# The modulation product of a two-block transformer step: TensorE beside the latent stage, or VectorE beside the feed-forward stage

## The reference, cut to what matters

```python
def _sq_relu_mlp(h, w_ff_in, w_ff_out):
    return jnp.square(jax.nn.relu(h @ w_ff_in)) @ w_ff_out
...
sil_c = jax.nn.silu(c)
sil_cc = jax.nn.silu(c_ctx)
mx = (sil_c @ w_ada[l] + b_ada[l])[:, None, :]
mc = sil_cc @ w_ada[l] + b_ada[l]
xsh1, xsc1, xg1, xsh2, xsc2, xg2 = jnp.split(mx, N_ADA, axis=-1)
csh1, csc1, cg1, csh2, csc2, cg2 = jnp.split(mc, N_ADA, axis=-1)
px = _split_in(_modulate(x, xsh1, xsc1) @ w_in[l])
pc = _split_in(_modulate(ctx, csh1, csc1) @ w_in[l])
```

## Time and profile before

| | us |
|---|---|
| median of 3 runs (4472.01 to 4479.48) | 4474.55 |
| span of the profiled execution, first to last instruction | 4370.0 |
| TensorE busy (84% of the span) | 3684.3 |
| VectorE busy (50%) | 2180.5 |
| GpSimd busy (27%) | 1195.4 |
| ScalarE busy (19%) | 846.3 |

### The profile page before, as it was taken

The page is one execution under the profiler, slowest core; times in us unless marked ns, Lnnn a source line. Parts: engine busy times, 40 slices in busy tenths (PEclk is TensorE's granted clock), DMA queues, the critical chain, the costliest instruction groups (busy, mean ns, idle before and its releaser), DMA issues.

```text
span 4370.0 us, 33503 instructions
## 1 busy us (share of the span) xinstructions
PE 3684.3 (84%) x10958; PEld 1877.5 (43%) x10958; DVE 2180.5 (50%) x4839; ACT 846.3 (19%) x1788; POOL 1195.4 (27%) x1151
## 2 busy tenths in 40 slices
PE   8788899899999799993999997476877678788787
PEld 4345564444445356542654456333433233233222
DVE  0547532310001356895652544885478778544443
ACT  1223321200003222113211122201122122111111
POOL 0200000000000000000000101335377777777775
PEclk9875758999999998995999998788999899999999
DMA  3340011122221111320122235677499999999998
GB/s 152 140 146 1 14 45 39 52 76 75 77 96 58 53 58 53 104 79 29 45 80 76 80 119 192 218 243 273 176 406 368 352 365 385 368 408 409 368 406 320
DMA packets 171916, 765.20 MB, mean 175 GB/s; under 512 B 19256, under 2 KB 19256, under 8 KB 160224
## 3 DMA queue, kind: packets, MB, share of 16 engines
q0 software_dynamic: 157904, 580.06, 35.2%
q1 hardware_dynamic: 13824, 182.97, 11.5%
q10 hardware_dynamic: 16, 0.02, 0.0%
HBM read 744.08 MB, written 18.89 MB: 175 GB/s over the span
## 4 chain that ended last, share of the span: by engine, by line
PE 49%; DVE 20%; POOL 9%; DMA 8%; issue 6%; ACT 3%; POOLq 0%; DVEq 0%; ACTq 0%
PE ps L252 13%; PE ps L258 9%; POOL arena L2589 8%; DMA arena<-in_pu,arena 5%; PE ps L1278 5%; PE ps L1336 5%; DVE arena L2619 5%; DVE arena L1422 4%; PE ps L2542 3%; PE ps L220 3%; PE ps L814 2%; PE ps L1560 2%; PE ps L832 2%; DMA arena<-in_pv,arena 2%; PE ps L1547 1%
## 5 line engine op out<-in xcount | busy, mean ns | idle before, releaser
L2542 PE MATMUL ps<-arena 128*128 128x512 f32 x2048 | 1001.8, 631 | 320.5 <-DMA arena<-in_pv,arena 159.3
L2619 DVE CUSTOM_DVE_ANT_0 arena<-arena 128x1024 f32<-128x1024 f32 x512 | 623.5, 1221 | 377.8 <-DMA arena<-in_pu,arena 376.7
L252 PE MATMUL ps<-arena 128*128 128x512 f32 (+1 forms) x1768 | 759.8, 590 | 31.4 <-ACT arena L2108 24.4
L2542 PEld LDWEIGHTS ps<-arena 128*128 128x128 f32 x2048 | 379.0, 197 | 925.4 <-issue 518.1
L2589 POOL DMA_INDIRECT arena<-in_pu,arena x512 | 540.6, 1056 | 372.3 <-issue 82.8
L2589 POOL DMA_INDIRECT arena<-in_pv,arena x512 | 545.4, 1065 | 193.3 <-issue 107.3
L258 PE MATMUL ps<-arena 128*128 128x512 f32 (+2 forms) x1408 | 527.1, 536 | 3.1 <-DVE arena L1251 0.9
L252 PEld LDWEIGHTS ps<-arena 128*128 128x128 f32 x1768 | 339.0, 193 | 437.4 <-issue 432.2
L220 PE MATMUL ps<-arena 128*128 128x128 f32 (+1 forms) x1094 | 218.1, 339 | 212.6 <-ACT arena L858 70.5
L258 PEld LDWEIGHTS ps<-arena 128*128 128x128 f32 x1408 | 267.8, 190 | 261.8 <-issue 219.4
L263 POOL TENSOR_TENSOR arena<-arena 128x1 f32<-128x1 f32 (+7 forms) x38 | 61.1, 1610 | 1106.8 <-DVE arena L675 396.7
(11 more groups left out here) (328 smaller groups left out, 3037.5 us busy)
## 6 DMA issues: line engine op xcount, KB each, us to landing
arena<-in_w_in SPq DMA_DIRECT2D x27, 2048.0 KB, 8.2
arena<-in_w_ada SPq DMA_DIRECT2D x12, 2048.0 KB, 8.1
arena<-in_w_ff_in SPq DMA_DIRECT2D x8, 2048.0 KB, 7.8
arena<-in_w_ff_out SPq DMA_DIRECT2D x8, 2048.0 KB, 8.0
arena<-in_w_pq SPq DMA_DIRECT2D x8, 2048.0 KB, 8.7
aside<-arena POOLq DMA_DIRECT2D x20, 512.0 KB, 5.9
arena<-in_w_at SPq DMA_DIRECT2D x4, 2048.0 KB, 8.0
arena<-in_w_o SPq DMA_DIRECT2D x4, 2048.0 KB, 8.2
```

Of the source, the lines that this page charges most:

```text
L252: x = t.matmul(PS[:, b, 0:n], hT[:, k, i * 128:(i + 1) * 128], w[:, k, :], start=k == 0, stop=k == nk - 1)
L2542: x = t.matmul(PS[:, b + c, :], DG[n % 4], row(f)[:, 512 * c:512 * c + 512], start=j == 0, stop=j == 127)
L2619: v.tensor_tensor_reduce(row(f), row(f), TT[i], 1.0, 0.0, ALU.mult, ALU.add, DOT[i % 2][:, j:j + 1]).then_inc(*pe.V.step("dot", 128 * i + j))
```

## The change

The product leaves latent and compress and is formed in `ffn`. The panels `w_ada` are loaded between the 12 first panels of the feed-forward layer, one after each. VectorE multiplies a panel with the condition and sums over the 8 blocks of rows: 8 instructions of 128 x 512 for a condition, two conditions for the first four panels, one for the other eight. TensorE then only sums over the 128 partitions, with a vector of ones: for the first four panels 8 products with 128 x 128 weights and 2 moving columns, for the others one product with 2 weight columns and 512 moving ones. The sums of panels 0 to 6 stand in TensorE's program in the middle of the next panel of the first weights, those of 7 to 11 among the second weights, in banks 4 to 7. The waits of the attention for the eight writes go to ScalarE's program after the relus. The sigmoid of the conditions stands before `gather(0)`.

```diff
-        ORDER = ([("w_in", c) for c in range(4)] + [("w_ada", c) for c in range(9)] + [("w_cmp", 0), ("w_cmp", 1)]
...
+        FF = [("w_ff_in", c) for c in range(8)] + [("w_ff_out", c) for c in range(8)]
+        ORDER = ([("w_in", c) for c in range(4)] + [("w_cmp", 0), ("w_cmp", 1), ("scratch", 0), ("w_xk", 0), ("w_xv", 0),
+                                                    ("w_out", 0), ("w_out", 1), ("w_xq", 0), ("w_xo", 0)]
+                 + [p for c in range(12) for p in (FF[c], ("w_ada", c))] + FF[12:]
...
                 if i < 3:
                     project(i + 1)
-                    drain(ada, 4)
...
         def compress_vector(v):
             wait_all(v, lt.P, lt.A, lt.V, lp.A, lp.V)
-            v.wait_ge(*ad.A.at("mod", 3))
-            o = PAR["bsh1"][0]
-            v.tensor_tensor(MOD, MOD, bc(PR[:, o:o + 16], 2), ALU.add).then_inc(*cm.V.step())
-            cm.V.own(v).tensor_scalar(MODf[:, 16:32], MODf[:, 16:32], 1.0, None, ALU.add).then_inc(*cm.V.step("mod"))
...
-        def compress_tensor(t, ada):
-            drain(ada, 1)
+        def compress_tensor(t):
...
             done("w_cmp", 1, cm.P)
-            drain(ada, 10)
             t.wait_ge(*cm.V.at("kc"))
...
         def attn_vector(v):
             wait_all(v, cm.A, cm.P, cm.V)
-            for s in s_row:
-                v.wait_ge(s, 64)
...
+        def ada_sums_tensor(t, c, banks):
+            t.wait_ge(*ad.V.at("acc", c))
+            b = bank(t, banks, ad.A, "row", c)
+            if c < 4:
+                for r in range(2):
+                    for k in range(4):
+                        x = t.matmul(PS[:, b, 8 * r + 2 * k:8 * r + 2 * k + 2], ADA[c % 2][r][:, 128 * k:128 * k + 128], cs("one")[:, 0:2],
+                                     start=True, stop=True)
+            else:
+                x = t.matmul(PS[0:2, b, :], cs("one")[:, 0:2], ADA[c % 2][0], start=True, stop=True)
+            x.then_inc(*ad.P.step("row", c))
...
+        def ada_sums_vector(v, c):
+            w = w3("w_ada", c)
+            v.wait_ge(*loaded("w_ada", c))
+            if c > 1:
+                v.wait_ge(*ad.P.at("row", c - 2))
+            for k in range(8):
+                ad.V.own(v)
+                for r in range(ada_conditions(c)):
+                    o, s = ADA[c % 2][r], SC[:, k, r:r + 1]
+                    if k == 0:
+                        v.tensor_scalar(o, w[:, k, :], s, None, ALU.mult).then_inc(*ad.V.step("acc", c))
+                    else:
+                        v.scalar_tensor_tensor(out=o, in0=w[:, k, :], scalar=s, in1=o, op0=ALU.mult, op1=ALU.add
+                                               ).then_inc(*ad.V.step("acc", c))
+            done("w_ada", c, ad.V)
+            if c == 4:
+                v.wait_ge(*ad.A.at("row", 3))
...
                     mm_feat(t, b, HT, 8, w3("w_ff_in", c), a, 512).then_inc(*ff.P.step("h", 4 * c + a))
+                    if c and a == 1:
+                        ada_sums_tensor(t, c - 1, BANKS)
...
+                        if c == 0 and i == 1:
+                            ada_sums_tensor(t, 7 + kk, (4, 5, 6, 7))
+                        if c == 0 and kk == 3 and i == 3:
+                            ada_sums_tensor(t, 11, (4, 5, 6, 7))
...
                 a.activation(AT[:, f, :], PS[:, held(ff.A, "h", f), :], ACT.Relu).then_inc(*ff.A.step("h", f))
+                if f > 4 and f % 4 == 1:
+                    ada_sums_scalar(a, f // 4 - 1)
+            for c in range(7, 12):
+                ada_sums_scalar(a, c)
+            for s in s_row:
+                a.wait_ge(s, 64)
+            a.wait_ge(*ad.V.at("mod"))
...
                 v.tensor_tensor(AT[:, f, :], AT[:, f, :], AT[:, f, :], ALU.mult).then_inc(*ff.V.step("h", f))
+                if f % 4 == 0:
+                    ada_sums_vector(v, f // 4)
+            for c in range(8, 12):
+                ada_sums_vector(v, c)
+            ad.V.own(v)
             add_x(0)
```

More of the change, by code:

```diff
@@ L274, in build @@
         LAT = take(2176)
-        RB = take(1024)
+        take(1024)
         LMF = A[:, U0 + 4160:U0 + 6080]
@@ L435, in build @@
         ad = stage("ada")
[L437 to L455, removed]
         def ada_scalar(a):
@@ L459, in ada_scalar @@
                 a.activation(SC[:, :, r], pr(n), ACT.Sigmoid).then_inc(*ad.A.step("sig", r))
[L460 to L475, removed]
         def ada_vector(v):
@@ L487, in build, with latent_tensor @@
         lt = stage("latent")
-        def latent_tensor(t, ada):
+        def latent_tensor(t):
             t.wait_ge(s_lat, 16)
@@ L524, in latent_scalar @@
             a.wait_ge(*lp.V.at("ki"))
+            ada_scalar(a)
             gather(0)
@@ L1224, in build @@
         AT = take(16384).rearrange("p (k n) -> p k n", k=32)
+        ADA = [[take(512) for _ in range(2)] for _ in range(2)]
+        RB = take(1024)
         s_cx = sem("s_cx")
@@ L1252, in modulated_vector, with ada_conditions @@
                                 ALU.add).then_inc(*ff.V.step(tag, k))
+        def ada_conditions(c):
+            return 2 if c < 4 else 1
+        def ada_sums_tensor(t, c, banks):
[9 more added lines that the diff above has]
+            x.then_inc(*ad.P.step("row", c))
@@ new lines, in ada_sums_scalar @@
+        def ada_sums_scalar(a, c):
+            a.wait_ge(*ad.P.at("row", c))
+            ps = PS[:, held(ad.A, "row", c), :]
+            if c < 4:
+                a.activation(MOD[:, 4 * c:4 * c + 4, :], ps[:, 0:16].rearrange("p (r f d) -> p f r d", r=2, d=2)[:, :, :, 0], ACT.Copy
+                             ).then_inc(*ad.A.step("row", c))
+            else:
+                o = RB[0:2, 512 * (c % 2):512 * (c % 2) + 512]
+                if c > 5:
+                    a.wait_ge(s_row[c % 2], 16 * ((c - 4) // 2))
+                a.activation(o, ps[0:2, :], ACT.Copy).then_inc(*ad.A.step("row", c))
+                a.wait_ge(*ad.A.at("row", c))
+                a.dma_start(ROWD[c - 4:c - 3, :], o[0:1, :]).then_inc(s_row[c % 2], 16)
@@ new lines, in ada_sums_vector @@
+        def ada_sums_vector(v, c):
[9 more added lines that the diff above has]
+                        v.tensor_scalar(o, w[:, k, :], s, None, ALU.mult).then_inc(*ad.V.step("acc", c))
+                    else:
+                        v.scalar_tensor_tensor(out=o, in0=w[:, k, :], scalar=s, in1=o, op0=ALU.mult, op1=ALU.add
[3 more added lines that the diff above has]
+                v.wait_ge(*ad.A.at("row", 3))
+                o = PAR["bsh1"][0]
+                v.tensor_tensor(MOD, MOD, bc(PR[:, o:o + 16], 2), ALU.add).then_inc(*ad.V.step())
+                ad.V.own(v).tensor_scalar(MODf[:, 16:32], MODf[:, 16:32], 1.0, None, ALU.add).then_inc(*ad.V.step("mod"))
@@ L2691, in tensor_program @@
             prep_tensor(t)
-            ada = ada_tensor(t)
-            latent_tensor(t, ada)
-            compress_tensor(t, ada)
+            latent_tensor(t)
+            compress_tensor(t)
             attn_tensor(t)
@@ L2710, in scalar_program @@
             prep_scalar(a)
-            ada = ada_scalar(a)
-            latent_scalar(a, ada)
-            compress_scalar(a, ada)
+            latent_scalar(a)
+            compress_scalar(a)
             attn_scalar(a)
```

11 lines of the change are left out of this document (2 added, 9 removed).

## The result

The changed kernel takes 4453.47 us in the median of 12 runs (4440.31 to 4466.24), the kernel before 4467.65 in 12 runs beside it (4448.50 to 4479.48). The ratio is 0.9963, 95% interval 0.9947 to 0.9979: 16.5 us, or 0.37%, faster; the two medians lie 14.2 us apart. The forecast was 15 us faster, with 4459 as the time.

A forecast was written before the change was run, and what follows sets the result against it. TensorE's product and a second chain through VectorE were taken to bound the latent stage, TensorE alone the feed-forward stage. 29.2 us gained less 14 paid gave -15 us, from 4474.55 to 4459; own range 4449 to 4468, wider range 4444 to 4477.

The forecast's parts named there:

- The removal: Latent and compress stages: without the product, line 993 starts 35.3 us earlier at unchanged clock, 29.2 after the clock's share.
- The clock's tax: Latent stage to line 920: TensorE's bursts start cold after idle time, taking back 6.1 us in sum.
- second path: Latent stage, T(1), project(3), gather(3): held no product, was cold before, stays 9.06 us long.
- second rival: Latent stage stays cold: 9 us gained, 14 to 22 paid, total 4480 to 4488; chance 0.10.
- The price in the feed-forward stage: TensorE never rests there, so added records cost full length: 6.4 us narrow, 6.9 wide, with turns 14.
- The loads: Feed-forward stage: two loads per panel of 27.8 us arrive in time with 9 us left; cost nothing.
- The attention's clock by windows: Attention: granted clock expected as before; a difference was named as a sign of being wrong.
- carried-over 104.6 us: Whole kernel: trace span lay 104.6 us under the runs' median; that gap was added to the changed span.
- the fifth: Feed-forward stage: each panel comes late behind its `w_ada`, 4 us over ten times, total 4499; chance 0.07.
- slow side of the attention: Attention: earlier, colder start keeps the clock at 0.50, up to 64 us more, half gives 4491; chance 0.05.
- The third: Rival: no clock penalty, a gain of 35 against 13 us, total 4452; chance 0.10.
- fast side of the attention: Attention: clock rises in the 139 us at 0.50; a third gained gives 4436; chance 0.06.

The follow-up runs named there:

- tight filler: Changed kernel plus idle matmuls leaving TensorE under 1.5 us idle before each T(i), the turning of tile i, and filling compress's gaps: 4335.83 us, ratio 0.9935.
- second chip: The changed kernel itself, run on another chip than the first comparison: 4350.57 us, ratio 0.9976 against the kernel before.
- seven panels: Against the changed kernel, seven product panels stay on TensorE in latent gaps, five go to VectorE, small fillers close gaps: 4333.28 us, ratio 0.9959.
- run without sums: Changed kernel without TensorE's sums over 128 partitions; ScalarE copies VectorE's partial sums, modulation not the reference's: 4337.75 us, ratio 0.9924 against the kernel before.
- kernel with moved waits: Kernel before, only the attention's starting waits for the eight row writes moved later, product left in place: 4367.96 us, ratio 0.9986.
- six panels: Against the changed kernel, six product panels stay on TensorE in latent gaps, six go to VectorE, no fillers: 4343.69 us, ratio 0.9943.
- loose filler: Changed kernel plus idle matmuls in TensorE's latent gaps, 17 after each of three projections and 8 before T(3): 4344.55 us, ratio 0.9957.

## Why the prediction was right, point by point

**What bounds.** Right. VectorE's chain took over as TensorE's panels left, and every T(i) of the changed kernel waits for VectorE. Line 642's counterpart begins 0.1 us after its operand (231.47 us), as said.

**The removal.** The predicted start of line 993 was 258 us, the traces say 254.8 and 256.4. From 0.7 to 0.9 us of this came in with the stages ahead (the first transposes at 124.4 and 124.6 instead of 125.3). So the step gave 31.1 and 29.7 us where 29.2 stood. Tile 3's wait of 5.28 us is gone, as said.

**The clock's tax.** The mechanism was right and is shown by the tight filler. Its 7.6 us are not the 6.1 of the sum, though: they also hold what T(1) and T(3) had paid in the kernel before. VectorE's wait along the second path is 9.06 us there and 7.70 with the tight filler, the wait at the end of T(3) 4.79 and 3.29. Without these 2.9 us the tax of the change on the second chip is 4.7.

Term by term, from T(0)'s start to the next squares the changed kernel takes 169.84 - 159.95 = 9.9 us where 7.5 stood warm: 2.4 instead of 1.9 (1.4 on the second chip). The second such path took 10.50 us (9.97 on the second chip) where I had counted nothing on top of 9.06, because the clock rose later inside the burst (T(1) and the projection after it take 4.08 and 4.76 us on the first chip, 3.52 and 3.83 before). Line 642's products paid nothing on one chip (7.15 us) and 1.7 on the other (8.81), against 1.9. Line 920's 16 records took 2.77 us, 1.2 more than the warm 1.54 where I had 2.3. The granted clock is 0.50 from the first of them to the last, so 2.77 is their cold length, and the 0.24 us each that I took from the earlier trace rows was not the cold rate of this burst. The sum is 5.0 on the first chip and 5.2 on the second. The errors have both signs, and that the sum came so near is partly luck.

The rule of the Trainium skill, in "TensorE: Matmul & The Clock Gate", "Part 1: The HAM clock gate", that the throttled clock is the default and activity releases it, agrees with the 2.15 us of the tight filler beside the 3.46 to 4.08 of the changed kernel; the gain near 9 us that it would have given if taken for each whole burst didn't come, since the clock rose within them. That it rises within every burst of over 4 us, as I wrote against the second rival, holds for the latent stage of before; in the attention's last tile TensorE is busy for 137.74 of 139 us and the clock stays at 0.50. So that sentence was no argument for other stages.

**The price in the feed-forward stage.** Forecast 14 us, measured 16.3. The narrow records took 0.105 us each (1.68 for 16, forecast 1.6), the pairs of wide ones 0.95 (0.86); with 4 x 1.68 + 8 x 0.95 = 14.3 two more microseconds lie in the pieces between, about 0.17 for each insertion where 0.06 stood. The kernel with seven panels separates the kinds: its five wide insertions lengthen the stage by 444.2 - 438.4 = 5.8 us, 1.16 each where 0.92 stood. Eight are 9.3, which leaves 1.76 for each group of narrow ones, where 1.66 stood. So the mis-sized term is the wide pair with its turns: 1.9 of the 2.3 us. VectorE worked 120 us in the stage (127 forecast; its first product of each sum took 0.485 us, the others 0.751). It was covered, as the run without sums shows.

**The loads.** Covered, as said. A `w_ff_in` panel behind its `w_ada` took 12.8 us to land in the median, 7.8 before, so some 15 of the 27.8 us were in hand where I had left 9. VectorE waited 77.3 us for panels. TensorE waited for VectorE only for the last squares ahead of the second weights, 3.7 us as before.

**What was not foreseen.** The attention's clock by windows was to be as before, and that it differed was named as a sign of being wrong. It does differ a little. Here is the changed kernel over the last tile, which before has 0.50:

```profile
508.00:646.00 138.00, 136.69 (x429) 89.58 (x430) 41.87 (x169) 38.81 (x90) 0.00 (x0) 0.54 0.11 46
```

The stretch from line 993 to the first relu is 3 to 4 us shorter in the changed kernel, on both chips. Its clock rises at the end of the half-speed stretch some 10 us earlier in relation to line 993. In the kernel with moved waits that doesn't happen (563.7 us), nor with seven panels (564.2), while with six panels (561.6) and, by some 5 us, with the tight filler (558.8) it does. The work there is the same in all of them. Why the clock rises at another place isn't settled; it wasn't tested by itself. With it the milestone balance on the first chip is 36.4 us gained up to the first relu, 16.3 paid, 20.1 left at the last addition.

**How near, and how much of it luck.** Four things lie between the forecast's 15 us and these 20.1: 0.9 us came in with the stages ahead, 1.9 more were gained in the latent stage, 4.4 came from the attention's clock, and 2.3 more were paid in the feed-forward stage. The total shows 16.5 of the 20.1, within the noise of the second block. So the mechanism was right and each of the two terms came within some 2 us, while a total that meets 15 us within 2 is luck in part. Of the 5.5 us between 4459 and 4453.47 none is the change's doing: the kernel before itself has a median of 4467.65 in its 12 runs, 6.9 us under that of the three runs that I started from. On the second chip 17.3 us stand at the last addition and 10.5 in the ratio.

**The carried-over 104.6 us** were wrong as a reading: they were the difference between two chips, except for some 2 us. The forecast was a difference added to the median, so the error cancelled. It would not have if a ratio of the span had been used.

**The rivals.** The cold latent stage (9 us gained), the fifth (late panels) and the slow side of the attention didn't come. The third, no clock penalty, is refuted by the tight filler. The fast side of the attention, forecast at 23 us, came from the change with 3 to 4 us, and in full only when it was provoked.

## What to carry to other kernels

Before moving filler work off an engine, follow the chain that waits behind it: of 82.8 us of TensorE's time only some 30 came back, and work that goes into a stage where the engine never rests costs its full length and the turns between kinds on top. Dense work between short bursts also keeps the clock up; if it goes, either size what stays to close the gaps, to about a microsecond in the two kernels here in which it helped, or reckon with bursts that begin at half speed. A better placement than either kernel's was to split the work: as many panels in the gaps as fit, the rest on the idle engine.

## What the runs showed of the hardware

- An engine that is never idle can run at half clock. In the attention's last tile of the kernel before TensorE is busy for 137.7 of 139 us at 0.50. One more wide product per unit raised the clock to 1.00 in the fourth unit and made the later ones 1.2 us shorter each, though there was more to do. The same product in the earlier tiles, among gaps, cost 1.87 us each while the clock was down, and there the clock rose only at 367 us, where without the product it was up by 330.
- Gaps of 0.9 to 1.8 us ahead of a burst left it at full speed (2.15 and 2.16 us for 18 transposes, in the tight filler, in seven panels and ahead of T(3) in the loose filler), gaps of 3.5 to 5.2 us did not (2.9 to 3.5 us, loose filler). The gap alone doesn't settle it: with 2.0 us ahead of T(1), behind a pause of 0.77 us and four small transposes, the kernel before took 3.52 us and the one with six panels 4.07.
- 16 records with 128 weight columns and 2 moving columns take 1.68 us, scarcely more than the 1.54 with 32 moving ones.
- Two chips of the same kind ran the same program in 4453 and 4351 us. The difference lies in the stretch of gathers from HBM (353 and 384 GB/s); its cause isn't shown.
